# Three stages of one-core fused transformer blocks reordered: attention's fills, the state part's preparations, and parts of an output projection

## What is computed

```python
for l in range(2):                                   # first_block
    h = rmsnorm(x, norm_mix[l]); proj = h @ w_in[l]  # aq ak av iq ik iw hq hf hi hg ga gb
    y_attn = dsa_attention(aq, ak, av, iq, ik, iw)   # 8 heads of 64; each query attends to its
                                                     # 128 best keys by an index score (top-k)
    log_f = logaddexp(log(lb), log1p(-lb) + log_sigmoid(hf)); k_in = -expm1(log_f)
    o = hgrn2_chunked(silu(hq), k_in, hi, log_f)     # S_t = diag(f_t) S_{t-1} + k_t v_t^T, o_t = S_t^T q_t
    y_hgrn = rmsnorm(o, hgrn_norm[l]) * silu(hg)
    x = x + (sigmoid(ga) * (y_attn @ w_pa) + sigmoid(gb) * (y_hgrn @ w_ph)) @ w_out[l]
    h = rmsnorm(x, norm_ffn[l]); g, u = split(h @ w_ffn_in[l]); x = x + (silu(g) * u) @ w_ffn_out[l]
# second_block, with 16 meta tokens as extra keys
out_a = softmax(qa ka^T / 8) va                      # 8 heads over 2 key heads
out_b = (softmax(qb1 kb1^T / 8) - lam * softmax(qb2 kb2^T / 8)) vb   # 4 differential heads
x = x + concat(out_a, rms_norm(out_b)) @ w_out_2; then an FFN as above
```

## Time and profile before

| | |
|---|---|
| three timed runs | 2288.53 us median (2285.6 to 2288.63) |
| the profiled execution | 2286.34 us, span 2284.5 us |
| PE busy | 2237.3 us (98%) |
| POOL busy | 1474.6 us (65%) |
| DVE busy | 1018.5 us (45%) |
| ACT busy | 619.7 us (27%) |
| mean granted TensorE clock | 0.997 |
| HBM | 90 GB/s over the span |

### The profile page before, as it was taken

One profiled execution on the slowest core, in us unless ns is written; L12 is line 12 of the kernel. 1 busy time (PEld: TensorE's weight loads), 2 busy tenths in 40 slices (PEclk: granted clock), 3 DMA queues, 4 the chain that ended last, 5 costly groups with the idle time before them and its releaser, 6 DMA issues.

```text
span 2284.5 us, 33352 instructions
## 1 busy us (share of the span) xinstructions
PE 2237.3 (98%) x12339; PEld 1800.0 (79%) x12339; DVE 1018.5 (45%) x1563; ACT 619.7 (27%) x1103; POOL 1474.6 (65%) x1452
## 2 busy tenths in 40 slices
PE   8999999999999999999999999999999989999999
PEld 7777777888888887777788888888886567888887
DVE  6965565533331149658555333311484554333200
ACT  4333434221110024344342211110334552111100
POOL 6654765876767766549668676767483246766763
PEclk9999999999999999999999999999999999999999
DMA  5321334323333333213343332332330103233322
GB/s 187 102 74 56 107 107 152 106 93 100 93 100 93 101 109 109 69 63 103 121 139 102 102 96 97 95 98 93 123 105 11 38 1 101 93 101 92 101 92 83
DMA packets 69871, 217.53 MB, mean 95 GB/s; under 512 B 8449, under 2 KB 10753, under 8 KB 69633
## 3 DMA queue, kind: packets, MB, share of 16 engines
q1 hardware_dynamic: 54016, 188.41, 26.5%
q10 hardware_dynamic: 15744, 27.52, 3.4%
HBM read 195.93 MB, written 10.49 MB: 90 GB/s over the span
## 4 chain that ended last, share of the span: by engine, by line
PE 86%; DVE 9%; ACT 3%; issue 1%; ACTq 0%; DMA 0%; POOL 0%; DVEq 0%; POOLq 0%
PE ps L1724 77%; PE ps L2221 1%; DVE score L1504 1%; DVE xl L1601 1%; DVE small L1500 1%; DVE xl L1584 1%; DVE b_sb L1579 1%; PE ps L1990 1%; ACT pe L1067 1%; PE ps L1975 1%; PE ps L2274 1%; DVE xl L1600 1%; PE ps L2003 1%; PE ps L2241 1%; DVE small L1387 1%
## 5 line engine op out<-in xcount | busy, mean ns | idle before, releaser
L551 POOL TENSOR_TENSOR w_lo<-w_raw,w_hi 128x512 fp32r<-128x512 f32 x700 | 959.9, 1371 | 58.4
L548 POOL TENSOR_SCALAR w_hi<-w_raw 128x512 fp32r<-128x512 f32 x700 | 493.6, 705 | 623.8 <-DMA w_raw<-wst 593.1
L1724 PE MATMUL ps<-h_hi,w_lo 128*128 128x512 f32 (+1 forms) x2056 | 804.4, 391 | 10.8 <-DVE h_lo L1169 2.7
L1724 PE MATMUL ps<-h_hi,w_hi 128*128 128x512 f32 (+1 forms) x2056 | 785.2, 382 | 0.0
L1724 PE MATMUL ps<-h_lo,w_hi 128*128 128x512 f32 (+1 forms) x2056 | 785.0, 382 | 0.0
L1724 PEld LDWEIGHTS ps<-h_hi,w_lo 128*128 128x128 f32 x2056 | 387.8, 189 | 109.1 <-issue 25.1
L1724 PEld LDWEIGHTS ps<-h_lo,w_hi 128*128 128x128 f32 x2056 | 387.9, 189 | 78.0 <-issue 6.7
L1724 PEld LDWEIGHTS ps<-h_hi,w_hi 128*128 128x128 f32 x2056 | 387.7, 189 | 75.4
L1724 PE MATMUL ps<-a_hi,w_lo 128*128 128x512 f32 (+1 forms) x572 | 213.7, 374 | 0.0
L1724 PE MATMUL ps<-a_hi,w_hi 128*128 128x512 f32 (+1 forms) x572 | 213.2, 373 | 0.0
L1724 PE MATMUL ps<-a_lo,w_hi 128*128 128x512 f32 (+1 forms) x572 | 213.2, 373 | 0.0
(11 more groups left out here) (304 smaller groups left out, 2500.1 us busy)
## 6 DMA issues: line engine op xcount, KB each, us to landing
w_raw<-wst SPq DMA_DIRECT2D x350, 512.0 KB, 3.6
rot<-raw ACTq DMA_DIRECT2D x70, 128.0 KB, 3.4
gates<-gt ACTq DMA_DIRECT2D x32, 256.0 KB, 3.8
stage<-gates ACTq DMA_DIRECT2D x32, 256.0 KB, 4.1
x_sb<-xin SPq DMA_DIRECT2D x8, 256.0 KB, 5.9
out<-x_sb SPq DMA_DIRECT2D x8, 256.0 KB, 4.6
kc<-cst ACTq DMA_DIRECT2D x1, 1056.0 KB, 6.4
kc<-cst SPq DMA_DIRECT2D x1, 417.0 KB, 8.6
```

Source lines behind the costliest of these rows:

```text
L548: eng.tensor_scalar(w_hi[s][:, part], w_raw[s][:, part], 1.0, 1.0, ALU.mult, ALU.mult)\
L551: eng.tensor_tensor(w_lo[s][:, part], w_raw[s][:, part], w_hi[s][:, part].bitcast(F32), ALU.subtract)\
L1724: m = eng.matmul(o, w, x, start=first and i == 0, stop=final and i == 2)
```

## The change

In words, by stage:

1. Attention: the fills alternate between banks 4 and 0. The scores are cut into blocks b: block 0 of the next pair stands between the transposes of blocks 1 and 2; block 1 comes after them, then two k's of the fill, then blocks 2 and 3, then the other six k's. Two rope steps now stand behind one top-k round, so that the last round has none behind it. The first score block waits for its own rope step alone, and no longer for tile `f3`.
2. State part: ScalarE computes both silus and the first decays before it copies `hv`; VectorE forms exponent 2 and weighs level 2 before the levels begin; level 0 waits for no `hv` tile. The gates are spread anew, with a table for each layer: level 0 comes after 0 (l = 0) or 1 (l = 1) gates, where it was 2.
3. Third block: the k's 3, 0, 1, 2 of `wo0..3` (16 products) move into steps 20 to 34, into bank 5, and are added to x by four extra VectorE instructions. GpSimd splits wo2 to wo5 in eight halves between the scalings of steps 18 to 25. The differential transposes now all use bank 4.

```diff
-GATE_STEPS = [[0, 1]] + [[2], [3], [4], [5], [6], [7], [8, 9], [10, 11]] + [[12], [13], [14], [15]]
+GATE_STEPS = ([[], [0], [1], [2], [3, 4], [5], [6, 7], [8], [9, 10, 11], [12], [13], [14], [15]],
+              [[0], [1], [2], [3], [4, 5], [6], [7, 8], [9], [10, 11], [12], [13], [14], [15]])
-            tile((l, n), i % 2 if i < 4 else 0)
+            tile((l, n), i % 2 if i < 4 else (4, 0)[i % 2])
+ROPES_BEHIND = ((3,), (4,), (5,), (6,), (7,), (8,), (9, 10), ())
+EARLY_ORDER = [(i, k) for i in range(EARLY) for k in (3, 0, 1, 2)]
+EARLY_AT = [20, 21, 23, 24, 25, 27, 28, 28, 29, 31, 32, 32, 33, 33, 34, 34]
+EARLY_ADDED = {25: 0, 29: 1, 33: 2, 35: 3}
...
+                        n = t - TB * PAIRS_A - 2
+                        if 0 <= n < 8:
+                            ahead = between + n // 2
+                            split(ahead, ahead % WSLOTS, 16 * (ahead // WSLOTS + 1), (n % 2,))
...
-                        taken(eng, (l, "hv2"))
-                        taken(eng, (l, "hv3"))
-                        for t in t_taken:
-                            eng.wait_ge(t, 16 * (l + 1))
                     else:
                         eng.wait_ge(lvx, 9 * l + i)
+                        if i == 1:
+                            taken(eng, (l, "hv2"))
+                            taken(eng, (l, "hv3"))
...
+                def scores_behind(p):
+                    scores(p, 1)
+                    if p == 0:
+                        eng.wait_ge(rope_done, 11 * (l + 1))
+                    else:
+                        eng.wait_ge(t_taken[0], 16 * l + 4 * p)
+                    fill(2 * p, range(0, 2))
+                    scores(p, 2)
+                    scores(p, 3)
+                    fill(2 * p, range(2, KT))
...
                 for p in range(PAIRS_1):
-                    transposes(p)
+                    transposes(p, 0)
+                    transposes(p, 1)
                     if p + 1 < PAIRS_1:
-                        scores(p + 1)
-                        fill(2 * p + 2)
+                        scores(p + 1, 0)
+                    transposes(p, 2)
+                    transposes(p, 3)
+                    if p + 1 < PAIRS_1:
+                        scores_behind(p + 1)
                         values(p)
-                        fill(2 * p + 3)
+                        fill(2 * p + 3, range(KT))
...
-                    if n:
+                    if t > TB * PAIRS_A:
+                        eng.wait_ge(t2_taken[1 - i], turn_of(t - 1, 1 - i) + 1)
+                    elif n:
                         eng.wait_ge(t2_taken[i], n)
...
+            def early(i, k):
+                if k == 3:
+                    begin((L2, f"wp{i}"))
+                    if i == 0:
+                        eng.wait_ge(t2_taken[1], turns_before(PAIRS_A))
+                c = half_chunk((L2, f"wo{i}"))
+                eng.wait_ge(ysp_lo, 8 * L2 + SPLIT_ORDER.index(k) + 1)
+                m = product(bank(5), *weights(c, k), h_hi[:, k, :], h_lo[:, k, :], k == 3, k == 2)
+                if k == 2:
+                    m.then_inc(acc_ready, 1)
```

More of the change, by code:

```diff
@@ L169, in weight_plan @@
             second_mixer(l)
+            for i in range(EARLY):
+                tile((l, f"wp{i}"), 5, False)
         for i in range(KT):
@@ L542, in _, with split @@
             rounds = len(chunks) // WSLOTS
[L544 to L547, removed]
+            def split(c, s, landed, halves=(0, 1)):
+                if halves[0] == 0:
+                    eng.wait_ge(w_dma[s], landed)
+                    eng.sem_inc(w_seen, 1)
+                for i in halves:
+                    part = slice(512 * i, 512 * i + 512)
                     eng.tensor_scalar(w_hi[s][:, part], w_raw[s][:, part], 1.0, 1.0, ALU.mult, ALU.mult)\
@@ L590, in _ @@
             softmax_weights()
-            done = between
+            done = between + 4
             splits(done, len(chunks))
@@ L829, in exps, with turned @@
                                        accum_out=small[:, 32 + n:33 + n]).then_inc(p_exp, 1)
-                def turned(p):
-                    for b in range(TB):
+                def turned(p, blocks):
+                    for b in blocks:
                         eng.wait_ge(t_ready[0], 16 * l + 4 * p + b + 1)
@@ L925, in moved, with state_values @@
                         step(ins) if at + 2 * w < P else ins.then_inc(lv_moved, 1)
-                decay(1)
+                def state_values(ts):
+                    for t in ts:
+                        free(eng.activation(hv_sb[:, t, :], acc((l, f"hv{t}")), ACT.Copy), (l, f"hv{t}"))
+                if l:
+                    state_values(range(1))
+                decay(1)
+                eng.activation(fl, fl, ACT.Exp, scale=-1.0).then_inc(prep_a, 1)
+                if l:
+                    state_values(range(1, TB))
+                decay(2)
+                if not l:
+                    state_values(range(TB))
                 gate_step(0)
                 for i in range(LEVELS + 1):
-                    decay(i + 2)
+                    if i:
+                        decay(i + 2)
                     if i > MASKED:
@@ L1508, in _ @@
                                 last[b] = step(ins)
-                    rope(3 + i)
+                    for r in ROPES_BEHIND[i]:
+                        rope(r)
                 for p in range(PAIRS_1):
@@ L1616, in _ @@
                 weigh(1)
-                for i in range(LEVELS + 1):
+                weigh(2)
+                for i in range(1, LEVELS + 1):
                     exponent(i + 2)
-                    eng.wait_ge(lv_mm, 8 * l + i + 1)
-                    if 0 < i <= MASKED:
+                    if i <= MASKED:
+                        eng.wait_ge(lv_mm, 8 * l + i + 1)
                         w = 1 << (i - 1)
@@ L1992, in values, with transposes @@
                     m.then_inc(y_ready, 1)
-                def transposes(p):
-                    for n in range(8):
-                        b, i = n // 2, n % 2
+                def transposes(p, b):
+                    if b == 1:
+                        taken(eng, filling(2 * p))
+                    for i in range(2):
+                        n = 2 * b + i
                         eng.wait_ge(p_norm, 32 * l + 8 * p + n + 1)
```

109 lines of the change are left out of this document (65 added, 44 removed).

## The result

| | before | after |
|---|---|---|
| timed runs | 2288.58 us median (2285.6 to 2290.76, 4 runs) | 2261.21 us median (2259.62 to 2261.82, 4 runs) |
| span of the profiled execution | 2284.5 us | 2259.1 us |
| PE busy | 2237.3 us | 2233.0 us |
| mean granted TensorE clock | 0.997 | 0.999 |

The ratio is 0.9883, 95% interval [0.9871, 0.9895]: 27 us faster. The forecast was 2261. The spans of the two profiled executions differ by 25.4 us where 27.2 were forecast. Attention fell short by 3.0 us; the two other parts and the program's start made up 1.2 of it.

A forecast was written before the change was run, and what follows sets the result against it. TensorE was taken as the bound, busy 2237.3 of 2284.5 us, so only idle time, drains and half clock could be won. Gains of 8.3 + 11.9 + 7.0 = 27.2 us gave a median of 2261 us, range 2252 to 2273.

The forecast's parts named there:

- A: Attention: reordered fills, scores and rope steps cover TensorE's waits; 8.3 us gained.
- drains: Attention: TensorE's pipeline emptying before a wait, claimed to cost 0.16 us beyond idle time for each of 19 waits.
- changes of kind: Attention: TensorE switching between kinds of matmul, 0.1 us each, about four more in each of six pairs; 2.0 us lost.
- B: State part: waits for level tiles and gate copies and a half-clock stretch go, one wait is added; 11.9 us gained.
- Rival 1: State part: the level chain is still VectorE's, B falls to about 7 us, 2266 us in all; chance 0.20.
- C: Third block: 16 products leave the last section, seven of them hidden in steps 31 to 34; 7.0 us gained.
- nine products: Third block: early products in steps 20 to 29, costing 7.1 us and replacing 3.6 of waiting, 3.5 net.
- contention: Third block: GpSimd's half splits slow VectorE's eight combinings by 0 to 1.0 us each; 0.6 us lost.
- Rival 2: Third block: differential steps become VectorE's, 8.6 us of new waits, C = -1.6, 2269.5 us; chance 0.12.
- 3: Attention: transposes wait for normalised rows because score blocks 2 and 3 are late; A halved, 2265 us; chance 0.08.
- 4: Third block: half splits between scalings delay VectorE, 4.0 us in each of eight steps, slower at 2293 us; chance 0.02.
- 5: Whole kernel: no effect, waits only change names and the three parts give back all; 2288 us; chance 0.02.

The follow-up runs named there:

- e9: The changed kernel with all eight attention fills in bank 0 again; one run, 2263.47 us.
- e6: The changed kernel with each pair's fill in one piece behind all scores; 2263.47 us, ratio 0.9898 to the kernel before.
- e7: The changed kernel with the old gate table in both layers; 2265.73 us, ratio 0.9909 to the kernel before.
- e10: The changed kernel with exponent 2 and the weighing of level 2 behind level 0; 2270.8 us, ratio 0.9922 to the kernel before.
- e11: The changed kernel with half splits in steps 18, 19 and 23 to 28 and, in layer 1, exponent 2 behind the scaling of f; 2259.92 us, ratio 0.9878.
- e8: As e7, with the copies of hv ahead of both silus, as in the kernel before; 2275.22 us, ratio 0.995 to the kernel before.
- e4: The changed kernel without half splits in the steps and with only eight early products; 2265.25 us, ratio 0.9905 to the kernel before.
- e3: The kernel before with only part 3 of the change (third block); 2281.90 us, ratio 0.997 to the kernel before.
- e5: The kernel before with the eight half splits alone, no early products; 2287.6 us, ratio 1.0002 to the kernel before.
- e12: As e11, with the first early product in step 19, the next seven one place earlier, one product in step 28; 2264.14 us, ratio 0.9894.

## Why the prediction was right, and where it was not

**Total and sign: right.** 25.4 us of span against 27.2. Launch-to-launch differences of the kernel before (2285.6 to 2290.76) made the medians agree to 0.2 us; that closeness is luck.

**A: the waits went as forecast, the size was 3.0 too large.** The forecast was 8.1 us of idle time, less 0.8 that comes back, plus 3.0 for drains (19 waits at 0.16), less 2.0 for changes of kind. Measured were 8.1, less 1.2 of waits left over, less 1.6 for drains and changes together: 5.3. The two waits for `pt_sb` in the first pairs were not foreseen. The rest, 2.6 us, is the net of two terms, forecast at +1.0 and measured at -1.6, and both were off the same way. The step that failed first is the reading of the earlier trace rows, "a wait costs its idle time plus 1.64 - 1.25 - 0.23 = 0.16". The 0.23 is the step inside a stream of like matmuls; from fill to scores it is 0.32 without any wait. So 0.09 of the 0.16 is a change of kind, which the change leaves in place. With 0.07 for 17 waits and 0.34 for the two inside fills (e9) the drains come to 1.9, with the 0.05 of the last pair to 1.5; e6 has 0.12 for the maxima. The second step is the price of the changes: the cut of a fill alone costs 0.22, 8 times, 1.8 of the 2.0, and the prediction counted six pairs and left out the two first ones. The scores that now stand between transposes come on top. How the 1.6 divides exactly, the runs don't settle.

**B: right.** All level and gate waits gone (9.7), and the half clock (a level and a gate of 1.84 and 7.78 us became 1.20 and 5.69: 2.7 us, as forecast). The added wait before level 0 came where the sum had put it, at 0.7 instead of 1.5. A new 0.3 at layer 1's cross stage was missed. In layer 0, where the clock is full in both kernels, five waits of 6.1 us idle brought 6.9, so there 0.16 per wait came out, though this too is a net of drains and a new order. Two bounds don't follow from their terms: B without the wait before level 0 is 11.9 + 1.6 = 13.5, not 13.8, and with 10.7 taken back it is 1.2, not 2; neither matters here. Rival 1, the chain still VectorE's, was wrong for the time, though right in that the chain has little to spare: e7, e10 and e11 each delay it, and each pays, 5.1, 1.3 and 1.1 us. Of the part's pieces the prediction priced only the whole; by e7 and e8 the gate table carries 5.1 us, and the silus' place 8.3 on top of the old table, half clock included.

**C: right in the sum, in part by luck.** The nine products cost 4.0 us in the steps, forecast 3.5 + 0.6. The contention is 0.9 of it (e4 and e11 agree) against 0.6, but not at the combinings, where the prediction priced it; it is at one `h_lo`. From step 31 on 11.3 were gained where 10.9 + 0.2 was forecast, and e3 gives the same -4.0, 11.3 and sum for the part alone. But 1.1 of the 11.3 is half clock that the prediction had no term for: behind the wait of 3.32 the kernel before needs 1.66 and 1.84 us for the values and the transposes that follow, at half clock, and e5 needs 0.99 and 1.38 for the same at full clock. Without this 10.2 would have been gained, by that estimate, and the seven products not hidden whole. Rival 2 (8.6 us of contention) is excluded by e5, with 2.1 at most.

**The other rivals.** 3: no transposes wait for normalised rows, though in the first pair VectorE's copy of a tile stands behind its normalising, and this is the wait for `pt_sb`. 4 and 5 are out by the result.

**The rule on the shared port.** The Trainium skill ("SBUF — State Buffer", on who interferes with whom) would let VectorE lose up to a whole GpSimd operation. The rows agree in size: `h_lo` takes 1.77 in the changed kernel, where it starts 0.4 us into GpSimd's two-input operation of 1.60, and 0.68 in e11 without it. By the rule taken at every combining C would have been -1.4; it was 7.3, because of eight combinings in steps 19 to 26 two lost 1.0 us, one 0.5 and the others 0.1 or nothing, and VectorE's slack took that.

**Not settled.** Which wait is followed by half clock: the same code has it in one kernel and not in the next. Why the wait for `pt_sb` is 0 in one kernel and 1.4 us in another with the same attention. And 0.5 us of the 25.4 lie before the first product.

## What to carry to other kernels

Price a wait that is to go by its idle time. What it costs beyond that was 0.05 to 0.12 us at most places here and 0.34 inside a run of products; and where a wait stands at a change of kind, first take off what the change costs without the wait (0.09 here). Cutting a run of products in two cost 0.22, and paid where it covered a wait of 0.57. Add up changes by stages, from the starts of the same instructions, rather than by medians: a stretch at half clock moves a total by 1.6 us in code that nobody touched. But look first how much a stage varies between kernels that share it. When work is put beside another engine's, list every two-input VectorE operation in those steps; the one that hurts may not be the one next to the edit.

## What the runs showed of the hardware

- Stretches at half the granted clock last 3.41 or 6.83 us in these traces, but for those at the very end. One of 3.41 us cost 1.6 in attention (e3, both layers), and 1.6 in the third block's first norm (from layer 1's first sum of squares to step 20, 687.6 us with it and 686.0 without). That norm, code that none changes, waits 1.9 us (2.3 in e5) in all fourteen kernels; ten have the stretch behind it, and e5, e7, e8 and e12 don't.
- A two-input VectorE operation of 0.68 us takes 1.76 us beside GpSimd's split, in three steps running; in e11, with the split gone from two of them, it takes 0.68 in these and 1.76 in the third.
- The FFN stages, untouched, take the same time to 0.1 us from kernel to kernel; the time up to the first product varies by 1.6 us (12.28 to 13.84), and attention of one and the same code by 1.6 us in a layer (81.3 to 82.9 from the first scores to the last values, at full clock).
